# Eight plain tiles ahead of the fast products in both feed-forward layers, with the activation mixtures spread over six of them

## The reference, cut to what matters

```
h = rmsnorm(x, norm_ffn[i])
x = x + (jax.nn.silu(h @ w_gate[i]) * (h @ w_up[i])) @ w_down[i]
```

## Time and profile before

| what | value |
|---|---|
| median of 3 runs | 1616.12 us (1615.8 to 1616.29) |
| the profiled execution | 1616.63 us, span of its instructions 1614.8 us |
| PE busy | 1588.7 us, 98% of the span, 8772 matmuls |
| DVE, ACT busy | 1023.3 us (63%), 706.2 us (44%) |
| mean granted clock of PE | 0.996 of full |
| layer 0: plain tiles, product tiles, down | about 199 to 271, 271 to 437, 439 to 560 us |
| layer 1: product tiles, down | about 792 to 957, 959 to 1080 us |

### The profile page before, as it was taken

How to read it: one execution, slowest core, us unless ns; L and a number is a source line. 1 busy time by engine, 2 the same in 40 slices (tenths; PEclk the granted TensorE clock), 3 DMA queues, 4 the chain that set the end, 5 groups by cost and what they waited for, 6 DMA issues and landing times.

```text
span 1614.8 us, 23766 instructions
## 1 busy us (share of the span) xinstructions
PE 1588.7 (98%) x8772; PEld 1330.8 (82%) x8772; DVE 1023.3 (63%) x1507; ACT 706.2 (44%) x1257; POOL 130.7 (8%) x121
## 2 busy tenths in 40 slices
PE   9999998999999999999899999999999999999998
PEld 7877887999888877777799988888777778888887
DVE  7666668777833366766877773337576667556444
ACT  6233434666722255553466663232355543233232
POOL 2000200000000000020000001123211111000000
PEclk9999999999999999999999999999999999999999
DMA  6422323333322251133333332334121121233332
GB/s 221 144 86 77 106 92 85 99 104 104 123 94 95 64 120 46 39 100 92 103 104 105 104 109 90 103 109 168 53 66 54 52 60 39 85 105 92 101 95 92
DMA packets 44750, 152.56 MB, mean 94 GB/s; under 512 B 5659, under 2 KB 8956, under 8 KB 44284
## 3 DMA queue, kind: packets, MB, share of 16 engines
q1 hardware_dynamic: 43888, 149.32, 29.8%
q10 hardware_dynamic: 780, 2.13, 0.5%
HBM read 149.04 MB, written 2.39 MB: 94 GB/s over the span
## 4 chain that ended last, share of the span: by engine, by line
PE 89%; DVE 7%; ACT 2%; issue 1%; DMA 0%; POOL 0%; SPq 0%; DVEq 0%; POOLq 0%; ACTq 0%
PE ps L2300 19%; PE ps L2302 18%; PE ps L2301 18%; PE ps L2506 7%; PE ps L2508 6%; PE ps L2507 6%; DVE w_lo L1358 1%; PE ps L2813 1%; PE ps L2835 1%; ACT w_hi L808 1%; PE ps L2801 1%; PE ps L2932 1%; PE ps L2933 1%; PE ps L2931 1%; DVE tmp L1393 1%
## 5 line engine op out<-in xcount | busy, mean ns | idle before, releaser
L1358 DVE TENSOR_TENSOR w_lo<-raw,w_hi 128x1024 fp32r<-128x1024 f32 (+3 forms) x192 | 251.0, 1307 | 165.7 <-ACT w_hi L808 165.0
L808 ACT ACTIVATE w_hi<-raw 128x1024 fp32r<-128x1024 f32 (+3 forms) x192 | 202.3, 1054 | 279.9 <-PE ps L2302 246.1
L2300 PE MATMUL ps<-a_hi,w_hi 128*128 128x512 f32 x632 | 255.6, 404 | 0.7 <-DVE t L1393 0.4
L2302 PE MATMUL ps<-a_hi,w_lo 128*128 128x512 f32 x632 | 246.9, 391 | 0.0
L2301 PE MATMUL ps<-a_lo,w_hi 128*128 128x512 f32 x632 | 246.4, 390 | 0.0
L2300 PEld LDWEIGHTS ps<-a_hi,w_hi 128*128 128x128 f32 x632 | 118.7, 188 | 32.5 <-issue 7.8
L2302 PEld LDWEIGHTS ps<-a_hi,w_lo 128*128 128x128 f32 x632 | 118.6, 188 | 25.9
L2301 PEld LDWEIGHTS ps<-a_lo,w_hi 128*128 128x128 f32 x632 | 119.0, 188 | 22.0
L2506 PE MATMUL ps<-mixed_hi,t_hi 128*128 128x256 f32 x384 | 109.3, 285 | 3.6 <-ACT ps L1031 3.5
L2508 PE MATMUL ps<-mixed_hi,t_lo 128*128 128x256 f32 x384 | 109.0, 284 | 0.0
L2507 PE MATMUL ps<-mixed_lo,t_hi 128*128 128x256 f32 x384 | 108.9, 284 | 0.0
(11 more groups left out here) (411 smaller groups left out, 3639.2 us busy)
## 6 DMA issues: line engine op xcount, KB each, us to landing
raw<-w SPq DMA_DIRECT2D x134, 512.0 KB, 3.6
raw<-w8b SPq DMA_DIRECT2D x70, 512.0 KB, 3.6
raw<-w_down SPq DMA_DIRECT2D x32, 704.0 KB, 4.1
w<-cmp_w SPq DMA_DIRECT2D x2, 2048.0 KB, 10.5
raw<-w_out_first SPq DMA_DIRECT2D x8, 320.0 KB, 2.8
raw<-w_nsa_o SPq DMA_DIRECT2D x8, 256.0 KB, 2.7
out<-o_t SPq DMA_DIRECT2D x8, 256.0 KB, 2.0
x<-xT SPq DMA_DIRECT2D x7, 256.0 KB, 6.0
```

Of the source, the lines that this page charges most:

```text
L808: act.activation(w_hi[:, slot, 0:w], raw[:, raw_slot, 0:w], ACT.Copy)\
L1358: dve.tensor_tensor(w_lo[:, slot, 0:w], raw[:, raw_slot, 0:w], w_hi[:, slot, 0:w].bitcast(F32), ALU.subtract).then_inc(w_lo_ready, 1)
L2300: pe.matmul(o, wh, a_h, start=start and at == 0, stop=False)
L2302: ins = pe.matmul(o, wl, a_h, start=False, stop=stop and at == kt - 1)
```

## The change

`PLAIN` goes from 6 to 8, so 16 plain tiles and 28 product tiles in the two layers stand where 12 and 32 stood. The four lots of mixtures are spread over plain tiles 1 to 6, and tile 7 is left for the weight sums of the first product tile. `halved` and `mixed` move to memory of their own, because the eight plain results take theirs. ACT rounds the next strip's weights ahead of the silu. The first strip of `down` gets a place of its own for its rounded weights (`far_hi`, `far_lo`), in memory that is free once product 1 of the last tile is done. In the last product tile PE runs product 4 ahead of product 7. The diff, cut to its core:

```diff
-PLAIN = 6
+PLAIN = 8
...
-    halved = at("halved", [P, 4, HS], F32, g0 + 2 * PLAIN * ROW)
-    mixed = at("mixed", [P, 4, HS], F32, g0 + (2 * PLAIN + 2) * ROW)
...
+    halved = at("halved", [P, 4, HS], F32, far + 2 * ROW)
+    mixed = at("mixed", [P, 4, HS], F32, far + 4 * ROW)
+    far_hi = at("far_hi", [P, SLOT], R32, far)
+    far_lo = at("far_lo", [P, SLOT], R32, far + 3 * ROW)
... ACT, ffn (gate is the silu, rounded writes g_hi_a, plain_high writes plain_ops)
+                for m in range(1, PLAIN - 1):
+                    split(n0 + 2 * m + 2, KT * P)
+                    gate(m)
+                    if m == 1:
+                        plain_high(0)
+                    if m == 3:
+                        mixed_high(1)
+                    if m == 4:
+                        plain_high(2)
+                    if m == 5:
+                        plain_high(3)
+                    split(n0 + 2 * m + 3, KT * P)
+                    rounded(m)
+                    if m == 1:
+                        mixed_high(0)
...
                 b11_high(layer, n0, 0, 0)
                 t12_high(layer, n0, 0, 0)
                 b22_high(layer, n0, 0, 0)
+                gate(PLAIN - 1)
                 t43_high(layer, n0, 0, 0)
+                qb = q0 + 2 * PLAIN
+                seeded_b(layer, qb, 0, 0)
+                rounded(PLAIN - 1)
+                seeded_g(layer, qb, 0, 0)
+                products(layer, n0, qb)
... ACT, end of products
-                act.wait_ge(blk_done, b + 2 * PRODS - 2)
+                n = b + 2 * PRODS
+                act.wait_ge(raw_in[0], (n // RAW + 1) * 16)
+                act.wait_ge(prod_done, 5 * PRODS * (layer + 1) - 4)
+                act.activation(far_hi[:], raw[:, 0, 0:SLOT], ACT.Copy).then_inc(w_hi_ready, 1)
+                seeded_c(layer, last, 1)
                 g_high(layer, PLAIN)
+                gate_first(layer, qb, last, 1)
                 g_high(layer, PLAIN + 1)
-                seeded_c(layer, last, 1)
-                gate_first(layer, qb, last, 1)
-                for m in range(PLAIN + 2, PLAIN + 8):
-                    g_high(layer, m)
                 seeded_d(layer, b, last, 1)
                 held(b, last, 1)
-                split(n, SLOT, 0, 0, (n // RAW + 1) * 16)
+                for m in range(PLAIN + 2, PLAIN + 6):
+                    g_high(layer, m)
                 gate_second(b, last, 1)
... DVE, ffn (gated multiplies gate and up, remainder writes g_lo_a)
+                for m in range(1, PLAIN - 1):
+                    n = n0 + 2 * m
+                    scaled(n, plain_bank(m, 0), tmp[:, 2 * (m % 2), :])
+                    split(n + 2, KT * P)
+                    if m == 1:
+                        normalised(layer, 0, g)
+                        mixtures(layer, 0)
...
+                    scaled(n + 1, plain_bank(m, 1), tmp[:, 2 * (m % 2) + 1, :])
+                    gated(m)
+                    split(n + 3, KT * P)
+                    remainder(m)
...
+                sums_first(layer, n0, 0, 0)
+                m = PLAIN - 1
+                scaled(n0 + 2 * m, plain_bank(m, 0), tmp[:, 2 * (m % 2), :])
+                b11_low(n0, 0, 0)
+                sums_last(layer, 0, 0)
+                t12_low(layer, 0, 0)
+                b22_low(n0, 0, 0)
+                scaled(n0 + 2 * m + 1, plain_bank(m, 1), tmp[:, 2 * (m % 2) + 1, :])
+                gated(m)
+                t43_low(layer, 0, 0)
+                remainder(m)
... DVE, end of products
+                dve.wait_ge(w_hi_ready, n + 1)
+                dve.wait_ge(prod_done, 5 * PRODS * (layer + 1) - 4)
+                dve.tensor_tensor(far_lo[:], raw[:, 0, 0:SLOT], far_hi[:].bitcast(F32), ALU.subtract)\
+                    .then_inc(w_lo_ready, 1)
... PE
-                        product7(layer, i, j)
-                        product4(layer, i, j)
-                        if not (end and j):
+                        if end and j:
+                            product4(layer, i, j)
+                            product7(layer, i, j)
+                        else:
+                            product7(layer, i, j)
+                            product4(layer, i, j)
                             product1(layer, b, i1, j1)
...
```

More of the change, by code:

```diff
@@ L957, in ffn @@
             def ffn(layer, n0, v, q0, r0):
[L959 to L984, removed]
@@ L985, in ffn, with gate, rounded @@
-                products(layer, n0, q0 + 2 * PLAIN)
-            def products_ahead(layer, n0):
+                def gate(m):
+                    act.wait_ge(lin_read, q0 + 2 * m + 1)
+                    act.activation(tmp[:, 2 * (m % 2), :], tmp[:, 2 * (m % 2), :], ACT.Silu).then_inc(silu_ready, 1)
+                def rounded(m):
+                    act.wait_ge(gu_ready, PLAIN * layer + m + 1)
+                    act.activation(g_hi_a[:, m, :], tmp[:, 2 * (m % 2) + 1, :], ACT.Copy).then_inc(g_hi_ready, 1)
@@ new lines, in plain_high, with mixed_high @@
+                def plain_high(k):
+                    act.wait_ge(sums_ready, SUMS * layer + 6 * k + 1)
+                    act.activation(plain_ops[:, :, 0, k, :], halved[:, 0:3, :], ACT.Copy).then_inc(t_hi_ready, 1)
+                def mixed_high(k):
+                    act.wait_ge(sums_ready, SUMS * layer + 6 * k + 4)
+                    act.activation(mixed_hi[:, :, k, :], mixed[:], ACT.Copy).then_inc(t_hi_ready, 1)
+                split(n0 + 2, KT * P)
+                spread(v, rstd[:])
@@ new lines, in ffn @@
+                split(n0 + 3, KT * P)
+                gate(0)
+                rounded(0)
+                for m in range(1, PLAIN - 1):
[13 more added lines that the diff above has]
+                        mixed_high(0)
+                    if m == 2:
+                        plain_high(1)
+                    if m == 4:
+                        mixed_high(2)
+                    if m == 5:
+                        mixed_high(3)
@@ L1597, in ffn @@
             def ffn(layer, n0, v, q0, g):
[L1599 to L1632, removed]
@@ L1635, in normalised @@
             def normalised(layer, k, g):
+                if k:
+                    dve.wait_ge(sums_ready, SUMS * layer + 6 * k - 1)
                 for t, rows in ((k, slice(0, 4, 3)), (k + KT // 2, slice(1, 3))):
@@ L1653, in mixtures, with plain_low @@
                                          ALU.mult, ALU.subtract).then_inc(sums_ready, 1)
+            def plain_low(layer, k):
                 dve.wait_ge(t_hi_ready, ROUNDED * layer + 2 * k + 1)
@@ L2277, in strip @@
                       ready=None, rows=P, late=None,
-                      aside=None, tiles=None, third=False, halves=False):
+                      aside=None, tiles=None, third=False, halves=False, far=False):
                 slot = n % 2 if slot is None else slot
@@ L2296, in strip @@
                         pe.wait_ge(ready[0], ready[1] + k + 1)
-                    wh, wl = (third_hi, third_lo) if third else (w_hi[:, slot], w_lo[:, slot])
+                    wh, wl = (third_hi, third_lo) if third else (far_hi, far_lo) if far else \
+                        (w_hi[:, slot], w_lo[:, slot])
                     wh, wl = wh[:, k * rows:(k + 1) * rows], wl[:, k * rows:(k + 1) * rows]
@@ L2582, in body @@
                         pe.wait_ge(lin_read, i * 2 + (q0 + j - 1))
-                        strip(n, None, None, j, kt=HALF, slot=0, stop=False, tiles=tiles[:HALF],
+                        strip(n, None, None, j, kt=HALF, slot=0, stop=False, tiles=tiles[:HALF], far=early,
                               ready=(g_lo_ready, FT * layer) if early else None)
```

62 lines of the change are left out of this document (48 added, 14 removed).

## The result

The changed kernel takes 1593.32 us (median of 4, 1592.64 to 1593.59) against 1616.16 us for the kernel before (median of 4, 1615.80 to 1616.29): 22.8 us less, a ratio of 0.9858 with a 95% interval of 0.9841 to 0.9875. Forecast were 1592.5 us, in a range of 1591.0 to 1598.5. The profiled execution took 1592.64 us, 24.0 under that of before.

What follows compares the result with a forecast made beforehand. PE was taken as the bound except at three places where it waits, plus half-clock stretches after stops. Terms summed to 12.6 us in layer 0 and 11.0 in layer 1: 1616.12 - 23.6 = 1592.5 us, range 1591.0 to 1598.5.

Steps and rivals of the forecast that it cites:

- (a): Plain tiles of the feed-forward part: no strip waits, a tile takes PE's 10.88 us; 5.47 us gained per layer.
- (b): Start of the products: product 3 no longer waits for ACT's copy after product 1; 2.33 us gained per layer.
- (c, e): Half-clock stretches go: within the products, 1.58 us in layer 0 only; at down's start, 1.60 us per layer.
- (e): Start of down: the half-clock stretch goes if the stop before it goes; 1.60 us gained per layer.
- (d): Last product tile and step to down: waits at product 5 and down go; 3.20 us gained per layer.
- the thinnest cover: Last product tile: ACT's copy for product 4 comes 0.5 us before it is due, the change's smallest spare.
- (f): Two product tiles per layer become plain tiles, 10.88 us each against 10.08; costs 1.60 us per layer.
- R1: A handoff keeps part of its wait, or a half-clock stretch stays or moves; 1594.1 to 1598.7 us, chance 0.20.
- R2: Plain tiles: DVE still binds them at 12.6 us a tile; 1608 us in all, chance 0.05.
- R3: The change fails at the handoffs and only (a) and (f) count; 1608.4 us, chance 0.04.
- R4: Plain strips: weights load too late for full pace, breaking even at 78 GB/s; slower kernel, chance 0.02.
- R5: Undisturbed products are paced by columns alone, 0.113 us a matmul, so the exchange costs more; 1594.7 us, chance 0.01.

Runs made afterwards that it cites:

- the repeat: The changed kernel run once more with no edit: 1593.24 us, ratio 0.9864 to the kernel before.

## Why the prediction was right, point by point

(a) **Plain stage, 5.47 a layer.** Right: product 1 starts at 287.03 (nine strips of 5.44 behind the 238.27 of the sum give 287.2), and the gate strips of tiles 2 to 7 start 10.88 apart. One sign was too strong: DVE's idle time before `w_lo` in a first half was to be gone, and 0.46 stayed, covered by PE's strip. The reason was the ring of two in-order queues, and the experiments narrow it: with both roundings first, and DVE's remainder of the weights ahead of that of the result, six tiles and unspread mixtures run at full pace too (no run separates ACT's order in the second half from DVE's). The spreading was needed for nothing here; without the order on ACT it is not enough. The prediction treated the waits on ACT as the cause and the spreading as a help, and left open how much each does.

(b) **Start, 2.33 a layer.** Right: 2.87 from product 1 to product 3, where 5.21 stood. The runs in between order the parts: 4.66 with the plain stage mended in both halves, 3.19 in the changed kernel with the start undone. So 0.55 came from the plain stage, 1.5 from a last tile without mixtures, and 0.3 from the order of sums and copies. The 1.5 is a difference between two kernels that differ in more than this, so its cause is argued; what shows the direction is that the copy's last input, the scaling of the up strip, came 2.2 us behind product 1's start in the one and 0.7 in the other.

(c, e) **Half clock, 1.58 and twice 1.60.** The stretches went. The working of (e) does not give its figure: 5 more matmuls at 0.2267 are 1.1 us. Two of the 10 in the window began outside the stretch, and 7 more than 8 make the 1.60. Measured, down went from 121.18 to 119.48 us, 1.70 less. But the terms are not constants of the kernel before. Its 25 executions in the three sets run from 1611.98, with a mean clock of 0.999, to 1617.04 with 0.996. Three stretches of 1.6 are about the size of this spread, and three other kernels with the same stops had them in some places and not in others (last section). I had subtracted all three from a median near the one profile, which showed all three. Against the medians of the three sets, 1615.05 to 1615.96, the gain is 21.7 to 22.7 us; that it came so near to 23.6 against the first median is in part luck.

(d) **End, 3.20 a layer.** Right: 7.20 from product 3 to down, and the new end alone gives 8.2 with the clock, 6.4 without. The far home with the old product order would have left 0.71 a layer; the thinnest cover was 0.75 where I had 0.5.

(f) **The exchange, -0.80 a tile.** Right: two plain tiles take 21.76 us and two product tiles 20.16 in the traces, 0.80 a tile. The medians say the same less sharply, 1.85 with a known wait of 1.3, and 3.8 without it, against 3.2 for four tiles. The rule of the Trainium skill ("TensorE: Matmul & The Clock Gate", section "Back-to-back issue gap"), by which the prediction's estimate was 1.19 a tile or 4.8 us in all, does not hold here: the distances between starts are 0.2267 and 0.12 in the new trace as in the old. The section gives its formula for a matmul by itself, and here every matmul has its own weight load.

By anchors: down starts 11.19 earlier in layer 0 (439.33 to 428.14) and 22.41 in layer 1 (959.14 to 936.73); the third stretch at half clock adds 1.6 behind that, in all 24.0, against 23.6 in the sum. From the first plain matmul to the end of down each layer lost 12.7 and 11.2, against 12.6 and 11.0. The median lies 0.8 above the forecast because the other executions of the changed kernel took 0.6 to 1.0 more than the profiled one, at a mean clock of 0.999 too. They have no trace, but the repeat's profiled execution is 0.8 longer as well, and its trace has only 0.1 of that ahead of the end of down in layer 1; 0.65 comes at one place of the second block (1303.78 us), where PE waits 0.71 for ACT's `k_tok` and did not in the first trace. So medians of these kernels can differ by 0.7 us for something outside the two layers.

Of the rivals, R1 did not come; R2, R3 and R4 were wrong, with PE busy in every window of the plain stage, and R5 by the 0.12 between starts among the products. (f) had the eight tiles as a cost; what the forecast did not ask is whether the rest of the change needs the room that they make. It does not: the change's headline is its one cost.

## What to carry to other kernels

When an engine at 98% busy still has stalls, measure its pace from the distance of starts, then look for rings: in two in-order queues that feed each other, as here, the waits add to the period (12.60 us a tile with a wait of 1.65, 11.56 with 0.61), so put the work that waits for nobody first in both, and check the sum of work and waits over a whole period, not the spare of each half. A rearrangement that makes room by giving up a cheaper algorithm should be tried without giving it up. Before buying slack, undo each part once: here six tiles with the new order, 1589.46 us, beat the eight.

## What the runs showed of the hardware that I had not expected

The stretch at half clock is not a fixed answer to a stop of PE. Five profiles have the same kinds of stop, and the granted clock behind them was:

| profile | first product 3 (gap 1.9 to 2.1 us), layers 0 and 1 | start of down (gap 2.1 us), layers 0 and 1 |
|---|---|---|
| kernel before | half, full | half, half |
| before, one half of the plain stage mended | half, half | half, full |
| before, both halves mended | full, full | half, full |
| before, new end | half, full | no stop |
| changed kernel, end undone | no stop | full, full |

In the first three the start of down follows a stop of 1.27 us at product 5, in the last one of 0.74; full clock came behind either. The plain tiles of the kernel before have gaps of 1.2 to 1.4 us every 12.6 us, with full clock throughout. One stretch of 6.8 us came in the second block, where no two matmuls ahead of it start more than 0.5 us apart, in the one of five executions that has a trace. A single profile of a kernel with such stops is therefore uncertain by 1.6 us for each of them.
